# Fourth layer's input projection of a two-stack transformer kernel in eight blocks of 386 columns instead of ten of 308

## What is computed

```python
def _mixer_cd(h, w_in, b_forget, rel_bias, w_out):
    proj = jnp.einsum('bsd,df->bsf', h, w_in)          # h: 256 x 1024, w_in: 1024 x 3080
    q_f, k_f, v_f, f_logit, q_c, k_c, v_c = _split_cols(proj, CD_SPLITS)   # 512 x3, 8, 512 x3
```

## Time and profile before

| what | us |
|---|---|
| median of three executions | 979.78 (979.6 to 980.25) |
| the profiled execution, its own time | 980.55 |
| its span from first to last instruction | 978.4 |
| TensorE matmul busy in the span | 948.9 (97%) |
| VectorE, ScalarE, GpSimd busy | 647.8, 474.4, 201.0 |
| first matmul of the projection starts, from the start | 656.71 |
| first instruction behind its last matmul starts | 726.88 |

### The profile page before, as it was taken

One profiled execution on the slowest core, in us unless ns is written; L12 is line 12 of the kernel. 1 busy time (PEld: TensorE's weight loads), 2 busy tenths in 40 slices (PEclk: granted clock), 3 DMA queues, 4 the chain that ended last, 5 costly groups with the idle time before them and its releaser, 6 DMA issues.

```text
span 978.4 us, 15120 instructions
## 1 busy us (share of the span) xinstructions
PE 948.9 (97%) x5588; PEld 792.4 (81%) x5588; DVE 647.8 (66%) x1184; ACT 474.4 (48%) x790; POOL 201.0 (21%) x188
## 2 busy tenths in 40 slices
PE   5999999999999999999999999999999999999996
PEld 2799666878886789878888888879997788888885
DVE  3657566975764775677767666676447776766665
ACT  1453577535445645583344444444458334444442
POOL 2015337203960401081000000010008100000001
PEclk9999999999999999999999999999999999999999
DMA  9864655434565247214475555535521446455441
GB/s 374 350 253 170 218 213 182 157 137 172 203 215 205 87 171 249 87 59 157 156 258 206 206 206 185 190 142 204 203 87 60 156 151 259 182 185 186 185 182 43
DMA packets 24103, 178.35 MB, mean 182 GB/s; under 512 B 3791, under 2 KB 4223, under 8 KB 7927
## 3 DMA queue, kind: packets, MB, share of 16 engines
q1 hardware_dynamic: 19840, 166.70, 46.1%
q0 software_dynamic: 2224, 8.94, 2.9%
q10 hardware_dynamic: 1991, 2.07, 0.8%
HBM read 176.65 MB, written 1.05 MB: 182 GB/s over the span
## 4 chain that ended last, share of the span: by engine, by line
PE 86%; DVE 8%; ACT 2%; DMA 2%; issue 1%; POOL 1%; SPq 0%; DVEq 0%; ACTq 0%; POOLq 0%
PE G L1323 12%; PE G L1325 12%; PE G L1324 12%; PE S L1443 8%; PE T L1443 8%; PE S L1442 4%; PE T L1442 3%; PE T L542 2%; PE G L1567 2%; PE G L1584 1%; PE G L1576 1%; PE T L637 1%; DVE wlo L2438 1%; DMA early<-in_ada_w 1%; PE G L455 1%
## 5 line engine op out<-in xcount | busy, mean ns | idle before, releaser
L2574 DVE TENSOR_TENSOR wlo<-ring,whi 128x2048 fp32r<-128x2048 f32 x88 | 154.4, 1759 | 88.4 <-ACT whi L2148 52.8
L1323 PE MATMUL G<-whi,hTh 128*128 128x308 f32 (+3 forms) x480 | 163.9, 341 | 0.5 <-DVE hTl L583 0.3
L1325 PE MATMUL G<-whi,hTl 128*128 128x308 f32 (+3 forms) x480 | 161.1, 336 | 0.0
L1324 PE MATMUL G<-wlo,hTh 128*128 128x308 f32 (+3 forms) x480 | 161.0, 335 | 0.0
L2438 DVE TENSOR_TENSOR wlo<-ring,whi 128x1024 fp32r<-128x1024 f32 (+3 forms) x66 | 105.4, 1636 | 65.2 <-ACT whi L1999 65.0
L1443 PE MATMUL S<-hT,whi 128*128 128x512 f32 x336 | 122.1, 397 | 0.0
L1443 PE MATMUL T<-hT,whi 128*128 128x512 f32 x336 | 120.6, 394 | 0.0
L1323 PEld LDWEIGHTS G<-whi,hTh 128*128 128x128 f32 x480 | 90.2, 188 | 11.4 <-DVE hTl L583 2.4
L2143 ACT CAST whi<-ring 128x2048 fp32r<-128x2048 f32 x44 | 83.9, 1907 | 26.5 <-PE S L1602 17.0
L1999 ACT CAST whi<-ring 128x1024 fp32r<-128x1024 f32 (+3 forms) x66 | 75.1, 1186 | 44.3 <-PE G L1325 30.1
L1324 PEld LDWEIGHTS G<-wlo,hTh 128*128 128x128 f32 x480 | 90.4, 188 | 5.7 <-issue 0.7
(11 more groups left out here) (429 smaller groups left out, 1876.3 us busy)
## 6 DMA issues: line engine op xcount, KB each, us to landing
ring<-in_ffn SPq DMA_DIRECT2D x44, 1536.0 KB, 6.5
ring<-in_dil_w_in SPq DMA_DIRECT2D x16, 1024.0 KB, 4.8
ring<-in_cd_w_in SPq DMA_DIRECT2D x10, 1232.0 KB, 5.4
ring<-in_ada_w SPq DMA_DIRECT2D x12, 1024.0 KB, 6.8
early<-in_ada_w SPq DMA_DIRECT2D x8, 1024.0 KB, 10.0
ring<-in_nsa_w_in SPq DMA_DIRECT2D x5, 1432.0 KB, 6.2
ring<-in_ab_w_in SPq DMA_DIRECT2D x4, 1440.0 KB, 6.9
vec<-in_vecs POOLq DMA_DIRECT2D x11, 512.0 KB, 5.4
```

The lines of the kernel that those rows point to most:

```text
L1323: pe.matmul(out_, act_h, w_h, start=first_, stop=False)
L1324: pe.matmul(out_, act_h, w_l, start=False, stop=False)
L1325: return pe.matmul(out_, act_l, w_h, start=False, stop=last_)
L2574: TT(wlo[b][:, part], ring[:, b, part], whi[b][:, part].bitcast(F32), ALU.subtract).then_inc(st[what + "_lo"], 1)
```

## The change

The 3080 columns are cut in eight blocks of 386 instead of ten of 308, after eight columns of zeros have been added at the end (8 x 386 = 3088). A block's row in a partition is then 8 x 386 = 3088 floats, so the slots of `ring`, `whi` and `wlo` grow from 3072 to 3088 floats. The second `whi` and `wlo` then reach 128 bytes beyond the attention operands; a tensor `slot_end` takes that place, and `oTl`, which lies over the end of the second `wlo`, moves by 64 bytes. The wait of VectorE for the forget columns becomes one for ceil(1544 / 386) = 4 blocks (before, 6 of 10). Every tensor behind the slots moves in SBUF by up to 384 bytes. Nothing in the order of the work is changed; loops over blocks run shorter.

```diff
-SLOT = 3072
+SLOT = 3088
...
-CD_C, CD_W = 10, 308
+CD_C, CD_W = 8, 386
...
         q2T = sb("q2T", [P, 8, T])
+        sb("slot_end", [P, 2 * SLOT - 3 * 8 * T])
         ring = sb("ring", [P, SLOTS, SLOT])
...
-        oTl = sb("oTl", [P, OUT_K, T], F32R, over="q2T", skip=4 * OUT_K * T)
+        oTl = sb("oTl", [P, OUT_K, T], F32R, over="q2T", skip=4 * OUT_K * T + 64)
...
-            dve.wait_ge(proj["cd_in"]["taken"], 2 * 6)
+            dve.wait_ge(proj["cd_in"]["taken"], 2 * -(-(1536 + 8) // CD_W))
...
-        "cd_w_in": tiles(v["cd_w_in_2"][0], CD_W), ...
+        "cd_w_in": tiles(np.pad(v["cd_w_in_2"][0], ((0, 0), (0, CD_C * CD_W - 3080))), CD_W), ...
```

More of the change, by code:

```diff
@@ L3214 @@
         "ab_w_ukv": tiles(v["ab_w_ukv_2"][0], 1024), "ab_w_out": half_items(v["ab_w_out_2"][0], OUT_W),
-        "cd_w_in": tiles(v["cd_w_in_2"][0], CD_W), "cd_w_out": half_items(v["cd_w_out_2"][0], OUT_W),
+        "cd_w_in": tiles(np.pad(v["cd_w_in_2"][0], ((0, 0), (0, CD_C * CD_W - 3080))), CD_W), "cd_w_out": half_items(v["cd_w_out_2"][0], OUT_W),
         "ffn0": ffn_steps(v["ffn_w_gate_2"][0], v["ffn_w_up_2"][0], v["ffn_w_down_2"][0]),
```

## The result

The changed kernel takes **986.69 us** (median of 6 runs, 985.28 to 987.65), the kernel before takes 979.94 (6 runs, 979.6 to 980.42) beside it. The recorded ratio is 1.0065, interval 1.0054 to 1.0075 (the quotient of the two medians alone is 1.0069). So it is slower by 6.7 us. The forecast was 980.9 in a range of 979.0 to 982.4, "within 0.2%" at 0.78. It was wrong, and by more than its range. The profiled execution took 987.23 us with a span of 985.1; before they were 980.55 and 978.4.

What follows compares the result with a forecast made beforehand. The prediction took TensorE, 86% of the chain, to bound the kernel. Its terms, -0.8 - 0.2 + 1.78 + 0.33 = +1.1 us, added to 979.78 gave 980.9 us, in a range of 979.0 to 982.4.

Steps and rivals of the forecast that it cites:

- What is covered: Side costs of wider blocks hidden behind other engines' work, some 0.3 us each if uncovered; slot layout counted 0, ±0.3.
- ends of all terms: The forecast sum with every term at its low or high bound: +0.6 to +2.1 us, 980.4 to 981.9 us.
- Rival D: Moved SBUF layout affects loads or operand reads in every layer, either sign; chance 0.05, half of it beyond 2 us.
- Fewer, wider matmuls: Fourth layer's projection on TensorE: 384 matmuls instead of 480, 4.20 us a group, a gain of 0.8 us.
- The small stall: TensorE's wait for `hTl` behind block 1, 0.34 us lost; six wider matmuls cover more of it, gain 0.2 us.
- rival B: Projection matmuls cost in proportion to width, 4.26 us a group; sum +2.1, 981.9 us; chance 0.05.
- Load, rounding, subtraction: Steps for block 1 ahead of GpSimd's rstd: 1.0 + 0.27 + 0.68 = 1.95 us later.
- The scaling: VectorE's scaling ahead of the projection, waiting for GpSimd's rstd: starts 1.78 us later, after 0.17 us of slack.
- `low_cd(0, 1)`: VectorE's own half block, ahead of the low part of x before the projection: 0.33 us later.
- Sum of the local part: Projection and the steps ahead of it: -0.8 - 0.2 + 1.78 + 0.33 = +1.1 us.
- Rival A: VectorE's wait for rstd ahead of the projection doesn't come; sum +0.1 to -0.7, down to 979.1 us; chance 0.12.
- Rival C: TensorE's clock falls to 1.2 GHz in the new gap before the projection; +3.0 to +5.0 us; chance 0.10.

Runs made afterwards that it cites:

- experiment 1: The changed kernel with its slots of 3088 floats, but ten blocks of 308 columns again: 984.50 us, ratio 1.0044 against the kernel before.
- experiment 2: The changed kernel, eight blocks, with slots of 3136 floats (a multiple of 256 bytes): 982.14 us, ratio 1.0017 against the kernel before; repeated, 981.86 us.
- experiment 4: The kernel before with 64 unused SBUF bytes ahead of `ring`, between `whi0` and `wlo0`, or behind `wlo0`: 984.06, 984.14 and 981.75 us.
- experiment 5: The kernel before with all its SBUF tensors moved by the same 64 bytes, no distance between them changed: 980.35 us, ratio 1.0004.
- experiment 3: Against experiment 2, ten blocks of 308 columns instead of eight of 386, slots still 3136 floats: 980.60 us, ratio 1.0001 against the kernel before.
- experiment 7: Against experiment 2, GpSimd makes rstd of token tile 0 before its subtraction instead of behind it: 983.86 us, ratio 1.0026 against the kernel before.
- experiment 8: Against experiment 2, GpSimd subtracts only the first quarter of block 1, VectorE the second quarter later: 980.33 us, ratio 1.0001 against the kernel before.
- experiment 4b: The kernel before with 64 unused bytes between `whi0` and `wlo0`, moving `wlo0`, `hTl` and all behind: 984.14 us, ratio 1.0042.

## Why the prediction was wrong, and where it was right

**The step that failed** is the last sentence of "What is covered": slots at multiples of 12352 bytes "cost nothing that I can find a row for; I count 0, with 0.3 to either side". It cost 4 to 5 us: 4.0 with ten blocks (experiment 1), 5.1 with eight (the changed kernel against experiment 2). A matmul of 512 columns went from 226.7 to 231.1 ns and more. Experiment 1 shows it with the slots alone, experiments 4 and 5 that distances do it, experiments 2 and 3 that a pitch on a raster of 256 bytes takes it away. The mistake was of method as much as of fact. The sentence bounded the cost by 0.3 us without any row. The trace of before holds none for it, because all these operands then lie at multiples of 256 bytes from each other. Where the trace shows nothing and the thing touches every instruction of the bound engine, a part of its time would have been the honest measure for the upper end: even 0.5% of TensorE's 948.9 us is 4.7 us. The 0.3 isn't in the prediction's "ends of all terms" either, and their lower end comes to +0.5 by its own terms, not +0.6.

**Rival D** ("the layout matters", chance 0.05, half of it beyond 2 us and left out of the range) came in. Its test, that "stretches of other layers have changed in length", is what the trace shows first. That "every layer would" take notice did not come true: it is the matmuls of 512 and 384 columns above all.

**Fewer, wider matmuls.** Forecast -0.8, with ends of -0.35 and -1.1. On the 256 raster (experiment 2) a group takes 4.23 us, the upper bound. A matmul is 176.4 ns, so its part beyond 160.8 for the columns is 15.6: near the 15.3 of the 358 columns, not the 13.4 of 308 and 512. I took the middle of two candidates; 358, the nearest row, would have been right. The small stall gave the 0.2 that was forecast (0.48 to 0.31 us between the two matmuls, the second figure with wider ones). The projection as a whole gained 0.65, where 1.0 was forecast. In the changed kernel itself the layout ate it: 4.27 us a group. That number would have confirmed rival B (a group of 4.26 or more), and experiment 2 shows that B is false. Two causes gave the mark of a third.

**Load, rounding, subtraction.** Issue to use of block 1 took 652.27 - 645.74 = 6.53 us in place of 5.75: +0.78, forecast 1.0. The rounding rose by 0.25 (forecast 0.27), the subtraction by 0.66 (0.68). All three come out a little under. The scaling started 1.54 us later against the statistics ahead of it, forecast 1.78. `low_cd(0, 1)` went from 1.44 to 1.77, +0.33 as forecast.

**Sum of the local part.** Forecast +1.1. Without the layout it measures +1.3 and +1.1 by stages (experiment 2 and its repetition) and +1.6 and +1.7 by medians. So the mechanism that the prediction spent its length on was right, and missed by 0.6 us at most. A little luck is in that: the lead-in cost less than forecast (1.95 and 1.76 for 2.11) and the projection gained less.

**Rival A** (no wait for rstd) is refuted by the 1.58 us in the trace. **Rival C** (the clock) did not come in the changed kernel: TensorE waited 1.3 us more and the granted clock is 1.00 in every stretch from 655 to 670 us. It did come in experiment 7, at this very place, behind a wait of 2.05 us, and cost 1.1 us. The length of the gap alone doesn't decide: near the start the same execution waits 2.06 us, and experiment 8's 2.29, and both keep the upper level. The prediction's "nothing shows where the fall would be" was a reading of slices that are too long for it: in the kernel before, too, the last 4 us are at 0.50.

## What to carry to other kernels

When a change resizes or pads a buffer, look first at a stretch that it does not touch and that the bound engine fills: the same instructions, start to start, before and after. Where wide matmuls are most of the work, keep the distances between their operands in SBUF on the raster on which they were, here multiples of 256 bytes, even at the cost of unused columns; if you can't, price it on the whole engine, not on the edited stage. Before a small result is moved ahead of a long one on GpSimd, look at what VectorE would then run beside the long one. And where a change makes TensorE wait, read the granted clock in stretches of a few us; forty slices of a long kernel hide a fall.

## What the runs showed of the hardware

- The distance in SBUF between the operands of successive matmuls sets their pace. With fp32r operands of 512 columns and a weight load for each, it was 226.7 to 227.1 ns with all distances on multiples of 256 bytes, and 229 to 234 ns with some of them 64 or 128 bytes off. Shifting everything by 64 bytes changed nothing (226.7). A moved operand is felt some eight matmuls beyond those that read it (experiment 4b).
- It does not strike all widths alike. With slots of 12352 bytes 386 columns lost 1.7 ns (178.1 against 176.4 in experiment 2) and 384 lost 2.2 (175.6 against 173.4), but 308, 358 and 360 moved by less than 1 ns on average (141.4 against 141.7, 163.7 against 164.4, 164.7 against 164.2). That is why the first layer's projection gave no sign of it, and the drift between the two timelines only sets in with the second's, at 216 us.
- VectorE's operation with two inputs in SBUF stood still while GpSimd's subtraction ran: 3.80 us for the pair in place of 1.54.
- TensorE's granted clock fell from 2.4 to 1.2 GHz in experiment 7, behind a wait of 2.05 us, and not behind waits of 1.1 to 1.4 us at the same place in other kernels with eight blocks, nor behind waits of 1.8 to 2.3 us near the start.

**What stays open.** What in the chip makes the distance matter was not found: the runs tell which distances are slow, not which access meets which. A trait of the widths may bear on it: the rows of a moving operand, one for each k-tile, start at multiples of 2048 bytes at 512 columns and of 1536 at 384, both multiples of 256, but at multiples of 1232, 1432, 1440 and 1544 at 308, 358, 360 and 386, where most rows lie off the raster in any layout. No run tests it. The gate and up matmuls of the feed-forward networks, in which the slot's columns are the stationary operand and x transposed passes through, got no slower in the changed kernel (means of 395 and 393 ns against 397 and 394), and I can't say why they are spared. Whether every multiple of 256 is fast was seen at two pitches only. Of the 1 us by which layout and blocks together exceed their sum, what the 386 columns don't explain was put down to scatter, and no run was made for it. At what gap the clock falls was not tested.
